# Moving the buffers that TensorE streams to another offset within 128 bytes, with every instruction kept in its place

## The reference, cut to what matters

```
# first block, twice
xn = rms_norm(h, norm_g[l])
(a_q, a_k, a_v, ..., gates, merge) = split(xn @ w_in[l])
branches = (dsa, mla, diff, sgu, memory)              # five mixers of width 512
mixed = sum(sigmoid(merge[n]) * ((o * silu(gates[n])) @ w_branch[l, n]) for n, o in branches)
h = h + mixed @ w_out[l]
# second block: 512 tokens and 256 context tokens
layer 0: neighbourhood attention (na_w_qkv, na_w_o), then swiglu(h, ffn_w_in, ffn_w_out)
layer 1: gated scan, eight heads (hg_w_in, hg_w_o), then swiglu
swiglu(h) = (silu(h @ w_a) * (h @ w_u)) @ w_out       # inner width 2816
```

## Time and profile before

| | us |
|---|---|
| runs of the kernel before | 4364.26, 4361.37, 4377.1 |
| median | 4364.26 |
| span of the profiled execution | 4369.1 |
| busy in it: TensorE (PE) | 3936.3 (90%) |
| VectorE (DVE) | 1683.2 |
| ScalarE (ACT) | 1444.4 |
| GpSimd (POOL) | 1394.0 |
| mean granted TensorE clock | 0.945 |

### The profile page before, as it was taken

How to read it: one execution, slowest core, us unless ns; L and a number is a source line. 1 busy time by engine, 2 the same in 40 slices (tenths; PEclk the granted TensorE clock), 3 DMA queues, 4 the chain that set the end, 5 groups by cost and what they waited for, 6 DMA issues and landing times. The chain is left out here.

```text
span 4369.1 us, 56680 instructions
## 1 busy us (share of the span) xinstructions
PE 3936.3 (90%) x22940; PEld 3344.9 (77%) x22940; DVE 1683.2 (39%) x3643; ACT 1444.4 (33%) x2330; POOL 1394.0 (32%) x517
## 2 busy tenths in 40 slices
PE   6899989999889998999989999999997888868998
PEld 5677878787767787878779887888886777757776
DVE  4825152322482514232351464211123756563111
ACT  3434242232243424223232463211113444432221
POOL 2121323333312132333322211222222656643333
PEclk8899999999889899999989999999998989979999
DMA  3131414333213142433312201112222111112332
GB/s 110 39 103 41 129 51 143 114 104 111 72 39 99 40 124 61 134 115 121 111 51 67 65 19 39 49 53 69 64 58 63 35 34 39 39 36 71 92 85 75
DMA packets 480271, 323.54 MB, mean 74 GB/s; under 512 B 31545, under 2 KB 476300, under 8 KB 480012
## 3 DMA queue, kind: packets, MB, share of 16 engines
q1 hardware_dynamic: 426304, 268.58, 21.3%
q10 hardware_dynamic: 53708, 51.33, 3.6%
HBM read 316.13 MB, written 2.16 MB: 73 GB/s over the span
## 5 line engine op out<-in xcount | busy, mean ns | idle before, releaser
L87 POOL TENSOR_TENSOR w_lo<-w_raw,w_hi 128x2048 fp32r<-128x2048 f32 (+6 forms) x329 | 1154.3, 3513 | 2655.5 <-ACT w_hi L235 2655.1
L235 ACT ACTIVATE w_hi<-w_raw 128x2048 fp32r<-128x2048 f32 (+3 forms) x278 | 471.8, 1698 | 1152.0 <-PE psum L279 1126.3
L277 PE MATMUL psum<-xF_hi,w_hi 128*128 128x512 f32 x1232 | 501.4, 407 | 61.8 <-POOL w_lo L87 20.0
L279 PE MATMUL psum<-xF_hi,w_lo 128*128 128x512 f32 x1232 | 491.9, 399 | 0.0
L278 PE MATMUL psum<-xF_lo,w_hi 128*128 128x512 f32 x1232 | 489.4, 397 | 0.0
L277 PE MATMUL psum<-ffn_h_hi,w_hi 128*128 128x512 f32 (+1 forms) x1056 | 380.3, 360 | 28.2 <-POOL w_lo L87 19.5
L279 PE MATMUL psum<-ffn_h_hi,w_lo 128*128 128x512 f32 (+1 forms) x1056 | 377.9, 358 | 0.0
L278 PE MATMUL psum<-ffn_h_lo,w_hi 128*128 128x512 f32 (+1 forms) x1056 | 377.5, 357 | 0.0
L277 PEld LDWEIGHTS psum<-xF_hi,w_hi 128*128 128x128 f32 x1232 | 237.3, 193 | 120.2 <-issue 50.0
L279 PEld LDWEIGHTS psum<-xF_hi,w_lo 128*128 128x128 f32 x1232 | 236.5, 192 | 54.1
L278 PEld LDWEIGHTS psum<-xF_lo,w_hi 128*128 128x128 f32 x1232 | 237.7, 193 | 50.2
(11 more groups left out here) (540 smaller groups left out, 8307.8 us busy)
## 6 DMA issues: line engine op xcount, KB each, us to landing
w_raw<-in_w_in_dram SPq DMA_DIRECT2D x54, 1024.0 KB, 5.3
ada_w<-in_ada_w_dram ACTq DMA_DIRECT2D x48, 1024.0 KB, 5.1
w_raw<-in_ffn_w_in_dram SPq DMA_DIRECT2D x88, 512.0 KB, 5.1
w_raw<-in_w_in_dram SPq DMA_DIRECT2D x82, 512.0 KB, 4.2
w_raw<-in_ffn_w_out_dram SPq DMA_DIRECT2D x32, 704.0 KB, 4.6
w_raw<-in_w_branch_dram SPq DMA_DIRECT2D x80, 256.0 KB, 4.5
w_raw<-in_hg_w_in_dram SPq DMA_DIRECT2D x32, 512.0 KB, 4.7
w_raw<-in_na_w_qkv_dram SPq DMA_DIRECT2D x12, 1024.0 KB, 5.1
```

The lines of the kernel that those rows point to most:

```text
L87: return eng.tensor_tensor(pair.lo, src, pair.hi.bitcast(F32), ALU.subtract)
L235: act.activation(self.w(j).hi, self.raw_w(j), ACT.Copy).then_inc(*self.high_done.up(1))
L277: pe.matmul(out, left.hi, right.hi, start=first, stop=False)
L279: return pe.matmul(out, left.lo, right.hi, start=False, stop=last)
```

## The change

Four sizes change, one argument is written otherwise, and one small buffer goes:

- `consts` grows from 1030 to 1038 floats;
- `row_gains` grows from 264 to 288 floats;
- `mem_rstd` gets 24 floats, of which the first two are used, as a slice that is passed on where the whole was sliced before;
- `hg_edge` (12 floats, decays that DVE reads in L2902 and L2904) lies now in the first 12 columns of the table `inv_freq` within `consts`.

```
-        self.wide = self.sb("row_gains", [P, 2 * P + 8], self.early)
+        self.wide = self.sb("row_gains", [P, 2 * P + 32], self.early)
-            norm = Norm(C, tmp, C.memF, mem, C.mem_g, None, C.mem_rstd[:, :], C.bank(7)[:, 0:MEM])
+            norm = Norm(C, tmp, C.memF, mem, C.mem_g, None, C.mem_rstd, C.bank(7)[:, 0:MEM])
-        C.mem_rstd = sb("mem_rstd", [P, 2])
+        C.mem_rstd = sb("mem_rstd", [P, 24])[:, 0:2]
-        startup(C, w, S, hF, spare, mod, small, C.mem_rstd[:, :])
+        startup(C, w, S, hF, spare, mod, small, C.mem_rstd)
-                edge=st("edge", [P, 2, 6]),
+                edge=C.inv_freq[:, 0:12].rearrange("p (d c) -> p d c", d=2),
-        consts = ctx.enter_context(nc.sbuf_tensor("consts", [P, NC + P + 2 + 6 + TT], F32))
+        consts = ctx.enter_context(nc.sbuf_tensor("consts", [P, NC + P + 2 + 6 + TT + 8], F32))
```

## The result

| | before | after |
|---|---|---|
| median, us | 4374.99 (4361.37 to 4379.9, 12 runs) | 4356.28 (4349.8 to 4366.65, 12 runs) |
| ratio after / before | | 0.9964, 95% interval 0.9953 to 0.9975 |
| span of the profiled execution | 4369.1 | 4364.8 |
| mean granted clock in it | 0.945 | 0.942 |

The change makes the kernel faster by 0.36%, which is 15.7 us of 4375 (10.9 to 20.6 by the interval). Forecast were 22.2 us. The time lies inside the range, but what happened is not the likeliest case: it is the rival that gives `xF` a loss. That 4356 is so near to the 4359 which the rival gave is luck: the forecasts count from the median of three runs, 4364.3, and the twelve have 4375.0. As a gain the rival had 5 us.

What follows compares the result with a forecast made beforehand. TensorE was taken to bound the kernel almost everywhere; gains of 14.5 + 3.5 + 2.0 + 2.2 = 22.2 us off the median of 4364.3 gave 4342 us. The range holding 8 in 10 was 4332 to 4364.5.

Steps and rivals of the forecast that it cites:

- the likeliest case: Whole kernel: the gains of all terms come as summed, 4342 us, own range 4334 to 4350; 64% chance.
- the rival that gives `xF` a loss: Period is 256 bytes: other buffers gain, `xF` matmuls lose 15.5 us moving and 1.5 us stationary; 4359 us, 14% chance.
- Where TensorE is the bound: TensorE, busy 90% of the span, sets the time almost everywhere, except where the next weights or scan tiles come last.
- nothing here turns on the clock: Steps of 229 to 234 ns at 512 columns are only possible at the clock's upper level, 2.4 GHz.
- 512 columns from 32 to 64, 14.5 us: 4320 matmuls of `ffn_h`, `ffn_g`, `hg_h`, `hg_og`, `na_oF` gain 4.2 ns each, 18.1 us, of which 14.5 on the path.
- the two deductions: Gains off the path: 2.0 us in swiglu of layer 1, 1.6 us for half of `hg_h` in the scan layer.
- `og`, 3.5 us: 960 matmuls of `og`, moving from 0 to 64 modulo 128, gain 3.6 ns each, all on the path.
- Activations as stationary operand, 2.0 us: Weights moving past activations: `na_x` gains 1.0 us, `hg_h`, `e_mem`, `b_cq` and `b_ckv` another 1.0; range 1 to 4 us.
- 256 columns moving, 2.2 us: Some 2100 matmuls of `ffn_h`, `ffn_g`, `hg_h`, `na_oF` gain 1.0 ns each; bounds 4.4 us gained or lost.
- `xF` keeps its rest modulo 128 and is put at nothing: `xF` stays at 64 modulo 128, so its matmuls were given no change, still 229.1 ns a step.
- No cost on the other engines, `ada_w` hidden: VectorE, ScalarE and GpSimd put at nothing; `ada_w` has 8.8 us for a landing in 5.1 us.
- The page weighed against the trace: Skill page's rule gives some 216 ns at 512 columns whatever the start address, so no change; the trace disagrees.

Runs made afterwards that it cites:

- both192: Changed kernel with 32 floats more in `row_gains` and in `mem_rstd`, so `xF` is back at 192 modulo 256 like the other streamed buffers; 4343.14 us, ratio 0.9923.
- repeats: `offsets` with the stationary operand at 128 only, each distance streamed twelve times behind a matmul of another width; 1667.7 us.
- offsets: Separate kernel without the computation: matmul streams for all 64 pairs of moving and stationary starts, 32 bytes apart modulo 256, at 512 and 256 columns; 1102.8 us.
- same_place: `both192` with 48 floats ahead of `og`, layer 1's `ffn_h` and `hg_og`, putting these and layer 1's `ffn_g` at distance 0 from the weights; 4343.1 us, ratio 0.9934.
- all_same: `both192` with `consts` laid ahead of the weights, so these too start at 192 modulo 256 and every product has distance 0; 4359.96 us, ratio 0.9976.
- both192_again: `both192` unedited, one more run on another chip; 4346.44 us.
- second_only: Second block as in the change; in the first, `xF` at 192 and `og` and the others at 0 modulo 256 as before; 4346.63 us, ratio 0.9931.

## Why the prediction was wrong

*Where TensorE is the bound.* Right. In `both192` TensorE is busy for 33.2 us less and the kernel takes 33.7 us less, and the waits stay. That "nothing here turns on the clock" holds for a step at the upper level, not for the time of one execution: after has 3.3 us less of busy time in its profile for 15.7 us less time by the medians, which goes with its longer stay at the lower level.

*512 columns from 32 to 64, 14.5 us.* Right, by a wrong name. `ffn_h` and `ffn_g` fell by 4.3 and 4.2 ns as forecast, `hg_h` by 3.3. With the counts of the earlier trace rows, 2112 x 4.3 + 1056 x 4.2 + 768 x 3.3 + 384 x 4.0 = 17.6 us, and 14.3 after the two deductions, which weren't tested by a kernel of their own. For the first of them the timeline of after has the sign that was named (as the earlier trace rows), first POOL's and then TensorE's row:

```profile
3987.79 4.60 POOL L87 TENSOR_TENSOR w_lo<-w_raw,w_hi 128x2048 fp32r<-128x2048 f32 x1 [7.86 <-ACT w_hi L235]
...
3992.44 0.51 PE L277 MATMUL psum<-ffn_h_hi,w_hi 128*128 128x512 f32 x1 [1.19 <-POOL w_lo L87]
```

The idle 1.09 us has become 1.19, by 24 x 4.2 ns = 0.1 us.

*`og`, 3.5 us.* Right: 960 x 3.5 ns = 3.4 us.

*Activations as stationary operand, 2.0 us, and 256 columns moving, 2.2 us.* The first is 2.4 us as a sum of parts that were sized wrongly: `na_x` gave 1.0 us as forecast, `hg_h` 4.8 ns a step (2.7 us) and `e_mem` 5.0 ns (0.9 us), and `xF` lost 0.9 ns (2.2 us). The second is 3.8 us, nearly all of it from `ffn_h`, 3.9 ns a step. Neither is a fixed price: these streams take one of two steps, 113.4 or 117.8 ns (`repeats`), so the rows of one execution could not bound them: `ffn_h`'s 3.9 ns lies outside the 2.1 ns that the prediction took as the most.

*The step that failed: "`xF` keeps its rest modulo 128 and is put at nothing".* Its 3696 matmuls went from 229.2 to 233.3 ns: 15.2 us in all, 12.7 us for the 3100 or so that lie in streams where no wait follows. The prediction took the period as 128 bytes. Its evidence was three starts, 64, 0 and 32 modulo 128, which were 192, 0 and 160 modulo 256; a period of 256 explains them as well. The rest modulo 128 was a name for "the place of `xF`", and the one buffer that left that place was `xF`. The rival named this, with its cost (15.5 us and 1.5 us) and its sign (`xF` above 231), at 14%. What was held against it, that `xF` was the fast one in both roles, at +64 and at -64 from the weights, was weak: at 256 columns both distances take either of the two speeds.

*The sum.* 14.3 + 3.4 + 2.4 + 3.8 less 12.7 is 11.2 us, and the steps of all long streams with their counts give 11.2 as well. The ratio says 15.7 (10.9 to 20.6). The rival had given 5: it put all 3696 matmuls of `xF` on the path (15.5 us for 12.7), and its terms at 256 columns come to 2.7 us where 6.2 came. The few us between 11.2 and 15.7 aren't accounted for; the choice that each stream makes at 256 columns, and the time at the lower clock, differ from one execution to the next. That 15.7 us is also what the likeliest case gave at its worst (15) is luck: the loss of 12.7 us, which it didn't have, was partly made up by the steps at 256 columns.

*No cost on the other engines, `ada_w` hidden.* Right. VectorE's operation of the earlier trace rows takes 748 and 747 ns, `ada_w` lands 0.1 us later.

*The page weighed against the trace.* The Trainium skill, "TensorE: Matmul & The Clock Gate", in "Back-to-back issue gap", has some 216 ns at 512 columns for a matmul by itself, and some 131 ns for a stream in which each matmul has a load of its own, which the prediction passed over; no start address stands in either. No run shows the one or the other: at a granted clock of 0.999 the steps are 226.8 to 234.3 ns (`offsets`), each with a load of its own, and the distance between the two operands sets which.

## What to carry to other kernels

Where TensorE is busy throughout, read the step of long streams from start to start, buffer by buffer, and set it against the distance between the moving and the stationary operand, modulo 256 bytes, not against an address alone. With a few floats of padding for each group of buffers, a moving operand of 512 columns goes 0 or 64 above the stationary one (227 and 229 ns against 233 or 234), and one of 256 columns goes to 64 or 192 (113.3 or 117.8 ns, whichever speed it takes), not to 0 or 96 (120); this kernel, which has both widths, was not shown to be faster anywhere than at 64 (`both192`). Short streams gain less: at distance 0 the first steps can be as slow as before (`same_place`). When a speed is explained by an address, list the other moduli that explain the same rows: whatever leaves the fast place in any of them is not at nothing.

## What the runs showed of the hardware

- The step of a stream with a new stationary operand for each matmul depends on where the two operands lie to each other: 226.8 to 234.3 ns at 512 columns, 113.3 to 120.0 at 256, with a period of 256 bytes (`offsets`, `repeats`).
- At the lower clock level the start made no difference: 426.7 ns for 512 columns of `xF` in before (distance 64) and in after (192), where the upper level has 229.2 and 233.3.
- The best distance at 512 columns, 0, is the worst at 256: 226.8 and 120.0 ns in `all_same`.
- At 256 columns and a distance of 64 or 192 a stream has two speeds, 113.3 and 117.8 ns, taken up at its start and kept, not fixed by the program (`both192_again`, `repeats`); at 160 it has 117.3 and 118.7 (`repeats`). At 512 columns and a distance of 64 a few streams did it, one of them of 86 matmuls (233.3 for 229.0, `second_only`).
- At 512 columns and distance 0 a stream can need some five steps of 229 to 236 ns before it runs at 227 (`same_place`).
